# Sample attention with matrix and weight roles exchanged, norm sums inside projections, and work moved off VectorE in the delta rule

## The reference, cut to what matters

```
h = rms_norm(x);  proj = h @ w_in                     # q, k, v, z, a, b, glu, gates
q, k, v = silu(causal_dwconv(qkv, width 4));  q, k normalised
o, state = gated_delta_rule(q, k, v, g, beta, state)  # 8 heads of 128x128
y_a = (rms_norm(o) * silu(z)) @ gdn_o
cv = causal_dwconv(glu_a * sigmoid(glu_b), width 31) + conf_conv_b
y_b = silu(layer_norm(cv)) @ conf_pw2 + conf_pw2_b
x += (sigmoid(g_a) * y_a + sigmoid(g_b) * y_b) @ w_out

q = rms_norm(x) @ xa_q                                # 4 heads of 256
# prompt rows: keys and values from mem_prompt @ xa_kv, 256 rows
# sample rows: each of 8 sequences has its own cache_mem_k, cache_mem_v (256 rows)
s = einsum("bthd,bmhd->bhtm", q, mk) * 256 ** -0.5
x += einsum("bhtm,bmhd->bthd", softmax(s), mv) @ xa_o

x += moe(rms_norm(x))                                 # top 4 of 32 experts, 1024 -> 2048 -> 1024
y = rms_norm(x)
```

## Time and profile before

| | |
|---|---|
| median of 3 runs | 1995.62 us (1993.2 to 1996.15) |
| the profiled execution | 1991.38 us, its span 1989.7 us |
| busy share of the span | PE 89%, DVE 40%, ACT 14%, POOL 9% |
| mean granted clock of TensorE | 0.917 of full speed |
| HBM, mean over the span | 252 GB/s |

### The profile page before, as it was taken

One profiled execution on the slowest core, in us unless ns is written; L12 is line 12 of the kernel. 1 busy time (PEld: TensorE's weight loads), 2 busy tenths in 40 slices (PEclk: granted clock), 3 DMA queues, 4 the chain that ended last, 5 costly groups with the idle time before them and its releaser, 6 DMA issues.

```text
span 1989.7 us, 27634 instructions
## 1 busy us (share of the span) xinstructions
PE 1763.9 (89%) x10243; PEld 1033.2 (52%) x10244; DVE 798.3 (40%) x1834; ACT 287.5 (14%) x663; POOL 170.7 (9%) x224
## 2 busy tenths in 40 slices
PE   5998998999999989978379999999998899899986
PEld 4766777778877667766333333333333333333332
DVE  2565789886543311241723222223322323322323
ACT  1332122222231001101000010001001001000001
POOL 2000124542110000001400000000000000000000
PEclk8997999999999898658579999999999999999998
DMA  7771763643332524236059999999999999999993
GB/s 174 151 114 37 97 98 67 103 94 111 101 119 86 190 94 139 85 129 230 0 220 403 417 418 418 417 419 418 417 419 417 417 420 417 417 419 417 418 419 147
DMA packets 146220, 501.86 MB, mean 252 GB/s; under 512 B 10641, under 2 KB 72498, under 8 KB 113216
## 3 DMA queue, kind: packets, MB, share of 16 engines
q1 hardware_dynamic: 138432, 482.37, 67.3%
q0 software_dynamic: 2704, 9.70, 1.7%
q10 hardware_dynamic: 5011, 8.79, 1.4%
HBM read 492.25 MB, written 9.43 MB: 252 GB/s over the span
## 4 chain that ended last, share of the span: by engine, by line
PE 23%; DMA 12%; SPq 9%; DVE 4%; issue 1%; ACT 1%; DVEq 0%
DMA ring<-in_moe_w 12%; PE bank L1022 11%; PE bank L1038 8%; SPq L1165 5%; SPq L1168 4%; DVE arena L2151 1%; DVE arena L2147 1%; DVE arena L2149 1%; DVE arena L2148 1%; PE bank L1063 1%; PE bank L1029 1%; ACT arena L1644 1%; PE bank L1064 1%; PE bank L1014 0%; PE bank L995 0%
## 5 line engine op out<-in xcount | busy, mean ns | idle before, releaser
L1022 PE MATMUL bank<-ring,arena 128*64 128x512 f32 x2048 | 474.8, 602 | 14.3 <-DMA ring<-in_moe_w 10.1
L1022 PEld LDWEIGHTS bank<-ring,arena 128*64 128x64 f32 x2048 | 140.2, 137 | 291.1 <-issue 218.8
L1038 PE MATMUL bank<-ring,arena 128*64 128x512 f32 x1024 | 248.3, 641 | 24.3 <-ACT arena L1644 24.3
L2196 DVE TENSOR_TENSOR xT<-xT,bank 128x288 f32<-128x288 f32 x256 | 99.0, 450 | 294.4 <-PE bank L1064 294.4
L588 PE MATMUL bank<-hT,ring 128*128 128x288 f32 x640 | 176.0, 418 | 0.4 <-ACT arena L1450 0.4
L1038 PEld LDWEIGHTS bank<-ring,arena 128*64 128x64 f32 x1024 | 78.0, 146 | 174.1 <-issue 171.3
L542 PE MATMUL bank<-hT,ring 128*128 128x288 f32 x512 | 135.5, 424 | 13.8 <-DVE hT L1692 13.8
L2192 DVE SCALAR_TENSOR_TENSOR arena<-bank,arena 128x512 bf16<-128x512 f32 x32 | 24.0, 751 | 292.7 <-ACT arena L1630 292.7
L588 PEld LDWEIGHTS bank<-hT,ring 128*128 128x128 f32 x640 | 117.6, 194 | 31.1 <-issue 4.4
L1792 DVE SCALAR_TENSOR_TENSOR ring<-arena,prm,ring 128x256 f32<-128x256 f32 x240 | 127.8, 595 | 1.1
L542 PEld LDWEIGHTS bank<-hT,ring 128*128 128x128 f32 x512 | 99.7, 198 | 48.7 <-DVE hT L1692 14.3
(11 more groups left out here) (361 smaller groups left out, 2131.7 us busy)
## 6 DMA issues: line engine op xcount, KB each, us to landing
ring<-in_moe_w SPq DMA_DIRECT2D x384, 1024.0 KB, 20.9
ring<-in_w_in SPq DMA_DIRECT2D x32, 1024.0 KB, 10.4
ring<-in_xa_kv SPq DMA_DIRECT2D x8, 1024.0 KB, 5.6
ring<-in_cache_mem_k SPq DMA_DIRECT2D x8, 1024.0 KB, 4.8
ring<-in_cache_mem_v SPq DMA_DIRECT2D x8, 1024.0 KB, 5.0
ring<-in_state_gdn POOLq DMA_DIRECT2D x8, 512.0 KB, 5.2
out_state_s<-ring POOLq DMA_DIRECT2D x8, 512.0 KB, 4.2
ring<-in_conf_pw SPq DMA_DIRECT2D x4, 1024.0 KB, 5.4
```

The source lines that it names most:

```text
L1022: last = mm(half_of(1 + q // 2, q % 2), x[:, k, :], ring[:, w_slot(k), 512 * q:512 * (q + 1)], start=False, stop=(k == KC - 1), skip_group ...
L1038: last = mm(half_of(b, n), act_T[:, f % 4, CAP * (f // 4):CAP * (f // 4 + 1)], ring[:, w_slot(KC + i), o:o + 512], start=(f == 0), stop=(f ...
L2196: tt(xT[:, c, :], xT[:, c, :], bank[SCATTER[c % 4]][:, 0:T], ALU.add).then_inc(scat_add, 1)
```

## The change

1. **Sample scores.** The queries become the stationary operand: `xq_pad` holds for every sequence a 128x32 tile per chunk, zero outside that sequence's 4 columns. The turned keys move, 256 columns. Each of 4 heads writes its own 32 rows of bank 6, and all 8 sequences accumulate into the same place. The scores come out with rows on the partitions, so `probs` needs no transposition before the softmax.
2. **Sample values.** The padded probabilities `pT_pad` are stationary (128x32 float32), V itself moves, 256 columns, float32. The split in bf16 parts and `values_low` are gone. The result has rows on the partitions and is copied to `xo_rows` and turned by two transposes. POOL clears both padded tiles once gdn_o is projected.
3. **Order of the attention.** `turn_probs` stands ahead of `turn_keys`, `attend` behind it, and DVE reads banks in an order that follows.
4. **Norm sums.** `project(..., sums=True)` for w_out and xa_o puts the sum over chunk n - 2 behind job n; ACT squares chunk k as soon as its residual is added.
5. **Delta rule.** `columns` (9 scalings for each head) and the copy ahead of `key_products` go from DVE to ACT. PE's fill after y now comes ahead of the special steps of the level (`w_s`, `wide_out` and others). The last head's fills are 1.0 instead of 1.6 us, and single side matmuls stand between the last `l2_sum`s.
6. **Sample rows of the convolution.** ACT makes 31 products for each of 8 chunks (128x32), up to five for each fill, with the bias in the first; DVE sums them by one reduction for each chunk, 128x32 results from 31 each. POOL's part is gone.

```diff
-        conf_acc = ring[:, 7, 0:256].rearrange("p (c b s) -> p c b s", c=KC, b=NB)
-        conf_sum = [ring[:, 7, 512 + SEQ * i:512 + SEQ * (i + 1)] for i in range(2)]
+        tap_rows = [ring[:, 7, NS * CW * i:NS * CW * (i + 1)].rearrange("p (n j) -> p n j", j=CW) for i in range(2)]
+        conf_sum = [SC[:, i, 0:SEQ] for i in range(2)]
...
+            def sum_square(k):
+                pe.wait_ge(sq_made, sq[0] + 1)
+                mm(bank[6][:, 0:T], ones[:, :], SC[:, sq[0] % 2, 0:T],
+                   start=(k == 0), stop=(k == KC - 1)).then_inc(sq_used, 1)
+                sq[0] += 1
...
+                        if sums and n >= 2:
+                            sum_square(n - 2)
...
+                part = SIDE if h < H - 1 else 1.0
...
+                    fill(part)
                     if l == 2:
-                        D_("columns")
+                        A_("columns")
...
-                    fill(SIDE)
                     A_(f"y{l}")
...
             for n in range(H):
                 l2_sum(n, H, 3)
-            fill(1000.0)
+                more(0.49)
+            more(1000.0)
...
-                for m in range(2):
-                    for h in range(XH):
-                        for c in range(XC):
-                            col = P * m + 16 * b + DT * h
-                            last = mm(bank[6][:, col:col + DT], kT_b[:, b % 2, XC * h + c, P * m:P * (m + 1)],
-                                      xq[:, XC * h + c, SEQ + DT * b:SEQ + DT * (b + 1)],
-                                      start=(c == 0), stop=(c == XC - 1))
+                for c in range(XC):
+                    for h in range(XH):
+                        last = mm(rows_of(h), xq_pad[:, b, XC * h + c, :], kT_b[:, b % 2, XC * h + c, :],
+                                  start=(b == 0 and c == 0), stop=(b == NB - 1 and c == XC - 1), skip_group_check=True)
...
+                for m in range(2):
+                    for h in range(XH):
+                        last = mm(rows_of(h), pT_pad[:, m, b, NS * h:NS * (h + 1)], wide(n)[:, m, ML * h:ML * (h + 1)],
+                                  start=(b == 0 and m == 0), stop=(b == NB - 1 and m == 1), skip_group_check=True)
...
-            for u in range(NU + 1):
-                if u < NU:
-                    scores(u)
-                    turn_keys(u)
-                if u:
-                    sample_scores(u - 1)
-                    attend(u - 1)
+            for u in range(NU):
+                scores(u)
+                if u:
+                    turn_probs(u - 1)
+                turn_keys(u)
+                if u:
+                    attend(u - 1)
+                    sample_scores(u - 1)
+            sample_scores(NB - 1)
+            turn_probs(NU - 1)
+            attend(NU - 1)
...
+                    for j in range(CW):
+                        out = tap_rows[c % 2].rearrange("p (b s) j -> p b s j", b=NB)[:, :, :, j]
+                        x = conf_hist[:, c, :, j:j + DT]
+                        if j == 0:
+                            A(out, x, ACT.Identity, scale=conf_w(j, c), bias=vec("conf_conv_b", c))
+                        elif j < CW - 1:
+                            A(out, x, ACT.Copy, scale=conf_w(j, c))
...
+                    if l == 1:
+                        step(act, g_dve, DVE_STEPS, h, "k_last")
+                        act.wait_ge(kv_turned, h + 1)
+                        for t in range(TT):
+                            last = columns(h, t)
+                        last.then_inc(g_act, 1)
...
+                        own(V.tensor_reduce(cvx[:, k, SEQ:T], tap_rows[k % 2], AX, ALU.add), conf_made)
```

More of the change, by code:

```diff
@@ L670, in _, with more @@
             SIDE = 1.6
-            def fill(us):
+            def more(us):
                 while us > 0:
@@ L678, in fill @@
                     us -= spent
+            def fill(us):
+                more(us)
                 mark[0] += 1
@@ L939, in _ @@
             for b in range(NB):
[L940 to L953, removed]
+                sample_values(b)
+            pe.wait_ge(xo_rows_made, 1)
+            for c in range(XC):
+                last = tp(bank[7][:, P * c:P * (c + 1)], xo_rows[:, P * c:P * (c + 1)], ident[:, :])
+            last.then_inc(xo_turned, 1)
             pe.wait_ge(xo_made, NU + 1)
-            project(J_XO, "xa_o", lambda k: xo[:, k, :])
-            sum_squares(6)
+            project(J_XO, "xa_o", lambda k: xo[:, k, :], sums=True)
             pe.wait_ge(norm_made, 5)
@@ L1224, in _ @@
             own(pool.memset(qkv[:, :, 0:GM], 0.0), pads_made)
[L1225 to L1246, removed]
-                if LEVEL_AT[h, l] >= DONE_AT["glu_a", KC - 1]:
-                    for _ in range(CW if LEVEL_AT[h, l] + 4 >= START_AT["mean", 0] else 2):
-                        next(rows_left, None)
             def load_states(h):
@@ L1928, in _ @@
                 own(tt(k_last_p, G["decay"][0:NS, 2, 0:NS], last_of[:, :], ALU.mult))
-                own(V.tensor_reduce(k_last, k_last_p, AX, ALU.add))
-                dve.wait_ge(kv_turned, h + 1)
-                for t in range(TT):
-                    last = columns(h, t)
-                own(last, g_dve, wait=False)
+                own(V.tensor_reduce(k_last, k_last_p, AX, ALU.add), g_dve, wait=False)
                 fill()
@@ new lines, in _, with read_keys, read_probs @@
+            for b in range(NB):
+                last = cp(xq_pad[:, b, :, DT * b:DT * (b + 1)], xq[:, :, SEQ + DT * b:SEQ + DT * (b + 1)])
+            own(last, xq_pad_made)
+            def read_keys(b, i):
+                read_bank(TR_KEYS + 4 * b + i, kT_b[:, b % 2, 0:4, P * (i // 2):P * (i // 2 + 1)], (4, P))
+            def read_probs(v):
+                dve.wait_ge(pt_done, v + 1)
+                if v >= 2:
+                    dve.wait_ge(xo_done, v - 1)
+                own(cp(probsT[:, v % 2], bank[2 + v % 2][:, 0:ML].rearrange("p (m n) -> p m n", m=2)), pt_made)
@@ new lines, in _ @@
+            NU = 2 * XH
+            for u in range(NU):
+                dve.wait_ge(scores_done, u + 1)
+                row_max(u, u % 2)
+                if u:
+                    read_probs(u - 1)
+                if u >= 2:
+                    dve.wait_ge(s_scores, u - 1)
+                read_keys(u, 0)
+                divide(u, u % 2)
+                read_keys(u, 2)
+            dve.wait_ge(s_scores, NB)
+            row_max(NU, 6)
+            read_probs(NU - 1)
+            divide(NU, 0)
@@ L2054, in _ @@
+            dve.wait_ge(pt_done, NU + 1)
+            for b in range(NB):
+                last = cp(pT_pad[:, :, b, :].rearrange("p m (h n) -> p m h n", h=XH)[:, :, :, DT * b:DT * (b + 1)],
+                          bank[7][:, 0:2 * P].rearrange("p (m h n) -> p m h n", m=2, h=XH)[:, :, :, DT * b:DT * (b + 1)])
+            own(last, pt_made)
             residual(J_XO)
```

795 lines of the change are left out of this document (401 added, 394 removed).

## The result

The median of 4 runs of the changed kernel is 1896.08 us (1894.92 to 1900.17), that of the kernel before on the same chip 1994.41 us (1985.31 to 1996.15). The ratio is 0.9523, 95% interval 0.9502 to 0.9544. The profiled execution took 1895.7 us, its span 1894.0 us; TensorE's mean granted clock is 0.948. Forecast were 1917 us, from 1900 to 1948 us: the time is 21 us under the forecast and 4 us under the range.

What follows compares the result with a forecast made beforehand. PE was taken as the bound nearly everywhere ahead of the expert loop, which DMA bounds at 417 GB/s. Savings 54 + 10 + 5.5 + 9 = 78.5 us off 1991.4 give 1912.9, plus 4.2: 1917 us, range 1900 to 1948 us.

Steps and rivals of the forecast that it cites:

- the term of the norm sums: w_out and xa_o: fewer products behind the last residual, 2 us each, plus xa_o's start clock; 5.5 us saved.
- the stretch behind it: From the norm sum of xa_o to the first expert, 73.3 us before: no saving forecast.
- the likeliest case: Whole kernel: the savings come as summed, 1917 us, own range 1900 to 1934 us; chance 0.66.
- the same pair in 2.84 or 5.67 us: Head loop's convolution: the same 7 DVE instructions take 2.84 us with POOL idle, 5.67 us beside POOL's sums.
- Attention: Attention stretch: new sample scores and full clock, unit 6.04 us, 51 us against 105.1 us; 54 us saved.
- The theory that the 4-column products pulled the clock down: Attention: with no product of 4 columns left, the unit was costed at full speed; the clock before was 0.65.
- The drain of the array: Attention: tiling mode changes twice in each unit; 16 drains of 0.24 us would add 4 us.
- Sample values: After the last attention unit: 16.1 us instead of 26.3 us with padded probabilities stationary; 10 us saved.
- Start of xa_o: xa_o begins at half clock, 3 us lost; half of that comes back with a busier stretch ahead.
- Delta rule: Head loop: PE's 12.0 us of listed waits for DVE go, 3 us of new waits; 9 us saved.
- ACT did not become the bound: Rival in the head loop: ACT late with y, 30 us, the gain there gone, 1956 us; chance 0.08.
- No rival: Rivals' chances: less overlap 0.11, clock at half 0.10, ACT 0.08, slower 0.03, gain not passed on 0.02.

Runs made afterwards that it cites:

- Experiment 1: Changed kernel, the norm sum of xa_o behind the whole projection again, w_out's stays inside: 1911.08 us, ratio to before 0.9601.
- experiment 5: Kernel before, each sequence's sample scores with 2 products of 16 columns instead of 16 of 4, the other 14 left out: 1951.49 us, one run, against 1987.41.
- experiment 6: Changed kernel, sample scores of all four heads in the same 32 rows of bank 6, one filling product ahead: 1917.57 us, one run.
- experiment 3: Changed kernel, POOL's load and split of the expert biases right behind the last sample scores: 1891.11 us, ratio 0.9491.

## Why the prediction was off

**The step that failed** is the term of the norm sums, "Saved: 5.5 us", together with the stretch behind it, which was left at nothing. It priced the products that leave the path and their wait, and these came as sized: 2.5 and 4.8 us for 2 and 3.5. It did not ask what DVE meets when it arrives 5 us earlier. The term's size is 7.3 + 11.4 = 18.7 us. Experiment 1 takes xa_o's sums out again and experiment 2 puts them alone into the old kernel; they move 14.2 and 13.6 us behind the start of xa_o, the sums' own time included. Without the 11.4 us the time would have been 1907.5 us, within the likeliest case's own range. The miss of 21 us is 17.2 us that the trace saved beyond the sum (95.7 for 78.5 us), and 3.8 us of the 4.2 that were added because the median before stood above the profiled execution: behind the change it stands 0.4 us above it. The sign was there to be read: DVE was busy for 50.23 us and POOL for 24.30 us in the window from 939.40, and the same pair in 2.84 or 5.67 us was used one paragraph further, for another stage.

**Attention: right.** 49 us for 51, a clock of 1.00, a unit of 6.0 for 6.04 us. A record of the sample scores takes 1.07 / 16 = 0.067 us, for 0.056 forecast and 0.069 (1.1 us for 16) with the start. The theory that the 4-column products pulled the clock down is borne out by experiment 5, only that with two products of 16 columns the clock was 0.90 and not full. No pause is visible where the tile width changes: L941 starts 0.99 us after L917, whose 8 records take 1.06 us, and L899 1.00 us after L941. The drain of the array that the Trainium skill names ("TensorEngine Tiling (Array Packing)", key properties) is not seen with a length that matters here.

**Sample values: right in kind, 3.5 us better.** Between the last unit and the first product lie 2.9 us where I took 4.2, and the 128 records take 8.8 us where I took 10.5. The clock fell not in the pause, as I had it, but behind it: the pause is at 1.00, and of the products' window at 0.83 the part to 812 us is at 0.63, that to 816 at 0.89 and the rest at 1.00.

**Start of xa_o: right.** 33.6 us for 34.6, at 1.00 instead of 0.91.

**Delta rule: the sum right, its working not.** I let PE's listed waits for DVE go, 12.0 us. Of these only 4.9 went. PE's longest waits in the changed kernel, up to gdn_o:

```profile
PE bank L844 <- ACT ring L2161: 6.4, 2, 4.1
PE bank L851 <- DVE ring L1575: 4.2, 1, 4.2
PE bank L808 <- DVE ring L1574: 2.9, 3, 2.1
PE bank L793 <- DVE ring L1547: 2.8, 1, 2.8
```

The wait of the earlier trace rows behind the masks (7.8 us) is 2.9 us here and that of 1.7 us is gone, but the one behind the last level grew from 2.5 to 4.2 us, and the one of 2.8 us, ahead of the first level, was 1.8 us before (it is not in the earlier trace rows). ACT did not become the bound: its wait is 6.4 us for 5.5. It has 182 us of work in 462, though a product of a tap costs 341 ns where I took 198. DVE's reductions cost 1.19 us each for 1.1, and its convolution stays at 532 ns on the mean. The 0.41 us of the forecast was a step and not a length: alone, seven take 2.84 us in both traces, and one lasts 0.48 us on the mean. Beside POOL's masks and copies, which remain, 63 of the 240 last 0.69 us; before, beside masks, copies and taps, 78 lasted 0.84 us. The 9 us show in PE's busy time. The window that answers to the first one of the changed kernel, in the kernel before:

```profile
183.00:654.14 471.14, 443.15 (x2343) 357.53 (x2341) 322.42 (x733) 105.78 (x213) 128.03 (x155) 0.97 0.44 96
```

As many matmuls are busy for 8.0 us less, and idle 1 us less. A clock of 0.98 instead of 0.97 on the mean goes with that. But it is no cause by itself: in experiment 5, whose head loop is that of before, PE was busy for 438.47 us, 4.7 us less than before, and gdn_o began at 654.1 us all the same. What is shown is that the taps' move brings 8 us up to gdn_o, of which 5.6 us are in the kernel's time; the columns' share, 2 us or so, is not clear of the noise. How the gain divides into fewer waits and a higher clock stays open.

**No rival came in.** The largest threat of the list, groups that don't overlap, is priced by experiment 6 at 21 us in the attention. All of them were for a slower kernel than the forecast; none was for a faster one.

## What to carry to other kernels

A shift of a few microseconds is worth more, or less, than its length wherever another engine's long instructions begin by a clock of their own. Before a stretch is left at nothing, look in it for instructions that last far longer than the same ones elsewhere (here eight of 0.44 us in 22.46 us), and find what stood beside them: moving that work (experiment 3) takes the gain without the luck of 0.4 us. And the price of small products is read with the clock of what surrounds them, not from their own rows alone.

## What the runs showed of the hardware

- VectorE was held for the length of GpSimd's instruction when it had two inputs in SBUF, or copied float32 from SBUF to SBUF (the changed kernel's trace): 1.95, 4.10 and 1.86 us for instructions of 0.26, 0.26 and 0.21 us. Beside the same GpSimd work, an instruction with one input from PSUM (L1694, 0.69 us, as in experiment 3 without it) and MAX8 (L1706, 0.20 us) went on undisturbed. The Trainium skill says this ("SBUF — State Buffer", SBUF: two separate sides): the two engines share a pair of ports by an exclusive lock, held for a whole instruction, which VectorE wants for two SBUF inputs, against a GpSimd instruction that reads SBUF, or in a 2-port mode. The trace agrees; the eight instructions of 22.46 us gave way to some eight of GpSimd's.
- Four groups of 32 columns overlap in both orders tried: 0.067 us for a float32 record of 256 columns against 3.64 / 16 = 0.228 us in one group, 3.4 times. The Trainium skill's figure for three groups, with 512 columns, is 2.38 ("TensorE: Matmul & The Clock Gate", part 3), 0.79 of the ideal; here it is 0.85.
- Products of 4 columns, each with a new 128x128 block, stood at a granted clock of 0.65 over the attention; with 2 of 16 columns for 16 of them it was 0.90, and in the new form 1.00.
